# Loading pairs of modulation weights two chunks later in a 1024-chunk weight stream

## What is computed

```python
s_lat = jax.nn.silu(c)
s_ctx = jax.nn.silu(c_ctx)
for layer in range(DEPTH_2):
    shift, scale, gate = jnp.split((s_lat @ ada_w[layer] + ada_b[layer])[:, None, :], 3, axis=-1)
    h = rms_norm(x, pre_g[layer]) * (1.0 + scale) + shift
    ...
    shift_c, scale_c, gate_c = jnp.split(s_ctx @ ada_w[layer] + ada_b[layer], 3)
```

## Time and profile before

| what | value |
|---|---|
| median of 3 runs | 3412.5 us (3409.27 to 3416.88) |
| profiled execution | 3413.3 us, of which the traced span is 3411.5 us |
| mean granted TensorE clock | 0.988 of full |
| PE busy | 3292.8 us, 97% of the span |
| DVE busy, ACT busy | 1537.0 us (45%), 1419.3 us (42%) |
| SP's transfers (queue q1) | 540.08 MB, 48.7% of the DMA engines' time |
| pairs' matmuls | between 590 and 2172 us, and a last block at 2414 us |

### The profile page before, as it was taken

One profiled execution on the slowest core, in us unless ns is written; L12 is line 12 of the kernel. 1 busy time (PEld: TensorE's weight loads), 2 busy tenths in 40 slices (PEclk: granted clock), 3 DMA queues, 4 the chain that ended last, 5 costly groups with the idle time before them and its releaser, 6 DMA issues.

```text
span 3411.5 us, 48332 instructions
## 1 busy us (share of the span) xinstructions
PE 3292.8 (97%) x20802; PEld 2859.4 (84%) x20802; DVE 1537.0 (45%) x1951; ACT 1419.3 (42%) x1962; POOL 32.7 (1%) x30
## 2 busy tenths in 40 slices
PE   7999998999999999999999999999799999999998
PEld 7989998689999987777777778788689888888886
DVE  5444445555555554446232222342544455453554
ACT  5444544544444444447321122232654444444443
POOL 0000002000000000000000000000000000000000
PEclk9999999999999999999999999999899999999999
DMA  6665544756666666665455555443423233232343
GB/s 207 184 189 174 153 151 157 256 189 227 220 225 206 216 227 246 230 231 185 144 173 169 172 171 170 154 141 101 131 81 105 88 102 108 92 106 91 101 136 118
DMA packets 349060, 556.97 MB, mean 163 GB/s; under 512 B 16880, under 2 KB 148976, under 8 KB 347696
## 3 DMA queue, kind: packets, MB, share of 16 engines
q1 hardware_dynamic: 346304, 540.08, 48.7%
q0 software_dynamic: 2256, 13.11, 1.0%
q10 hardware_dynamic: 288, 0.70, 0.1%
HBM read 551.60 MB, written 2.23 MB: 162 GB/s over the span
## 4 chain that ended last, share of the span: by engine, by line
PE 54%; ACT 5%; DVE 4%; issue 2%; DMA 0%; DVEq 0%; ACTq 0%
PE ps L675 48%; PE ps L700 2%; ACT whi L1049 1%; PE ps L868 1%; PE ps L890 1%; ACT hA L1224 1%; PE ps L872 1%; DVE hA L1804 1%; PE ps L886 1%; ACT L1224 1%; DVE hA L1796 1%; DVE wlo L1568 0%; DVE hB L1793 0%; DVE hB L1791 0%; PE ps L731 0%
## 5 line engine op out<-in xcount | busy, mean ns | idle before, releaser
L1568 DVE TENSOR_TENSOR wlo<-raw,whi 128x1024 fp32r<-128x1024 f32 x819 | 999.7, 1228 | 1503.5 <-ACT whi L1049 1496.0
L1049 ACT ACTIVATE whi<-raw 128x1024 fp32r<-128x1024 f32 x824 | 861.8, 1058 | 1395.7 <-PE ps L675 710.6
L675 PE MATMUL ps<-HCh,whi 128*128 128x512 f32 (+1 forms) x1664 | 606.3, 364 | 2.1 <-DVE HCl L1639 2.1
L675 PE MATMUL ps<-HCl,whi 128*128 128x512 f32 (+1 forms) x1664 | 595.3, 358 | 0.0
L675 PE MATMUL ps<-HCh,wlo 128*128 128x512 f32 (+1 forms) x1664 | 595.0, 358 | 0.0
L675 PE MATMUL ps<-Vh,whi 128*128 128x256 f32 x1408 | 403.6, 287 | 12.9 <-DVE wlo L1568 12.8
L675 PE MATMUL ps<-Vh,wlo 128*128 128x256 f32 x1408 | 398.2, 283 | 0.0
L675 PE MATMUL ps<-Vl,whi 128*128 128x256 f32 x1408 | 398.2, 283 | 0.0
L675 PE MATMUL ps<-whi,HCh 128*128 128x256 f32 (+1 forms) x1152 | 377.2, 327 | 1.6 <-DVE HCl L1666 1.5
L675 PEld LDWEIGHTS ps<-HCh,whi 128*128 128x128 f32 x1664 | 316.3, 190 | 71.2 <-issue 21.6
L675 PE MATMUL ps<-wlo,HCh 128*128 128x256 f32 (+1 forms) x1152 | 368.3, 320 | 0.0
(11 more groups left out here) (301 smaller groups left out, 4088.5 us busy)
## 6 DMA issues: line engine op xcount, KB each, us to landing
raw<-in_ada_w SPq DMA_DIRECT2D x192, 512.0 KB, 5.7
raw<-in_w_up SPq DMA_DIRECT2D x176, 512.0 KB, 5.1
raw<-in_w_in SPq DMA_DIRECT2D x160, 512.0 KB, 3.7
raw<-in_od_w_in SPq DMA_DIRECT2D x160, 512.0 KB, 3.5
raw<-in_ev_w_in SPq DMA_DIRECT2D x96, 512.0 KB, 6.2
raw<-in_w_down SPq DMA_DIRECT2D x88, 512.0 KB, 5.1
raw<-in_w_out SPq DMA_DIRECT2D x32, 512.0 KB, 5.2
raw<-in_w_ple_gate SPq DMA_DIRECT2D x32, 512.0 KB, 3.8
```

The source lines that it names most:

```text
L675: mm = e.matmul(o, a, b, start=first and t == 0, stop=last, skip_group_check=True)
L1049: e.activation(m.whi[ch.i % SPLIT][:, 0:n], m.raw[ch.slot][:, 0:n], ACT.Copy).then_inc(S("hi"), 1)
L1568: e.tensor_tensor(m.wlo[ch.i % SPLIT][:, 0:n], m.raw[ch.slot][:, 0:n], m.whi[ch.i % SPLIT][:, 0:n].bitcast(F32), ALU.subtract).then_inc(S( ...
```

## The change

The stream no longer has a pair right behind the main chunk it belongs to. `Plan.group` holds the pair back and appends its two chunks to the stream once two more main chunks have been appended (`LATER = 2`). TensorE still multiplies it where it did. The blocks (`fill`) stay where they were. A split chunk's place is now three split chunks ahead, whatever the stream position, except where the buffer it will use (that of chunk c - 5) held an ada or a raw chunk: then it isn't placed earlier than the main chunk behind which TensorE uses that old chunk (`behind`; for a raw chunk that is the raw chunk itself). The places are now on main chunks alone, so ACT and DVE no longer look for splits at pairs. Two turns of the modulation vectors (`ADA_LAG = 3`, small transposes) are now counted in main chunks rather than in stream positions, two chunks later.

```diff
-ADA_LAG = 3
+ADA_LAG, LATER = 3, 2
...
-    def chunk(self, src, kt, cols, split):
+    def chunk(self, src, kt, cols):
         ch = Chunk()
-        ch.c, ch.src, ch.kt, ch.cols = len(self.chunks), src, kt, cols
+        ch.src, ch.kt, ch.cols, ch.i = src, kt, cols, None
+        return ch
+
+    def stream(self, ch, split=False, behind=None):
+
+        ch.c = len(self.chunks)
         ch.slot, ch.landed = ch.c % RING, 16 * (ch.c // RING + 1)
+        ch.behind = behind or ch
         if split:
...
             at = self.splits[ch.i - AHEAD].c if ch.i >= AHEAD else 0
-            ch.place = -1 if ch.i < 2 else max(at, ch.c - (RING + len(self.filling) - 1))
-        else:
-            ch.i = None
+            old = self.chunks[ch.c - RING] if ch.c >= RING else None
+            ch.place = -1 if ch.i < 2 else max(at, old.behind.c if old and old.i is None else 0)
         self.chunks.append(ch)
-        return ch
...
             rows = W[j * kt * 128:(j + 1) * kt * 128, c0:c0 + cols]
-            at = len(self.chunks)
-            G.chunks.append(self.chunk(rows.rearrange("(k p) c -> p k c", p=128), kt, cols, not raw))
+            ch = self.chunk(rows.rearrange("(k p) c -> p k c", p=128), kt, cols)
+            G.chunks.append(ch)
+            self.stream(ch, not raw)
+            self.mains += 1
+            while self.held and self.held[0][0] <= self.mains:
+                for x in self.held.pop(0)[1].chunks:
+                    self.stream(x, behind=x.behind)
             if fill and j == 2:
-                G.fill = self.ada(fill, at)
-                self.filling = [ch for u in G.fill for ch in u.chunks]
+                G.fill = self.ada(fill)
                 for u in G.fill:
+                    for x in u.chunks:
+                        self.stream(x, behind=G.chunks[0])
                     self.count(*u.chunks)
                 self.count(*G.chunks)
...
-            G.after.append(self.ada(int(self.due), at))
+            G.after.append(self.ada(int(self.due)))
+            self.due -= int(self.due)
             for u in G.after[-1]:
                 self.count(*u.chunks)
-            self.due -= int(self.due)
-            G.turns.append([b for c, b in self.later if at >= c])
-            self.later = [(c, b) for c, b in self.later if c > at]
-        self.filling = []
+                for x in u.chunks:
+                    x.behind = ch
+                self.held.append((self.mains + LATER, u))
+            G.turns.append([b for c, b in self.later if self.mains >= c])
+            self.later = [(c, b) for c, b in self.later if c > self.mains]
...
     def units(self, units):
         for u in units:
-            for ch in u.chunks:
-                self.splits(ch.c)
             self.ada(u)
```

More of the change, by code:

```diff
@@ L68, in __init__ @@
         self.units, self.limit, self.products = 0, 0, 0
-        self.filling, self.later = [], []
+        self.held, self.later, self.mains = [], [], 0
         self.pool_every = 0
         self.n_lo = {"dve": 0, "pool": 0}
-    def chunk(self, src, kt, cols, split):
+    def chunk(self, src, kt, cols):
         ch = Chunk()
-        ch.c, ch.src, ch.kt, ch.cols = len(self.chunks), src, kt, cols
+        ch.src, ch.kt, ch.cols, ch.i = src, kt, cols, None
+        return ch
+    def stream(self, ch, split=False, behind=None):
+        ch.c = len(self.chunks)
         ch.slot, ch.landed = ch.c % RING, 16 * (ch.c // RING + 1)
+        ch.behind = behind or ch
         if split:
@@ L116, in group @@
             elif not fill or j > 2:
-                self.count(G.chunks[-1])
+                self.count(ch)
             self.due += 0 if j in quiet else self.rate
-            G.after.append(self.ada(int(self.due), at))
+            G.after.append(self.ada(int(self.due)))
+            self.due -= int(self.due)
             for u in G.after[-1]:
                 self.count(*u.chunks)
-            self.due -= int(self.due)
-            G.turns.append([b for c, b in self.later if at >= c])
-            self.later = [(c, b) for c, b in self.later if c > at]
-        self.filling = []
+                for x in u.chunks:
[3 more added lines that the diff above has]
+            self.later = [(c, b) for c, b in self.later if c > self.mains]
         G.done = G.chunks[-1].n
@@ L134, in count, with ada @@
             ch.n = self.products
-    def ada(self, n, at):
+    def ada(self, n):
         made = []
@@ L149, in ada @@
             u.chunks = [self.chunk(self.W_ada[l][i * 256:(i + 1) * 256, m * 512:(m + 1) * 512].rearrange(
-                "(k p) c -> p k c", p=128), 2, 512, False) for i in (2 * u.j, 2 * u.j + 1)]
+                "(k p) c -> p k c", p=128), 2, 512) for i in (2 * u.j, 2 * u.j + 1)]
             if u.last and u.batch < 2:
-                self.later.append((at + ADA_LAG, u.batch))
+                self.later.append((self.mains + ADA_LAG, u.batch))
             made.append(u)
@@ L492, in chunks @@
                 self.pump()
-            if j == 2:
-                self.behind(G.fill)
             self.units(G.after[j])
@@ L498, in chunks @@
         return G
-    def behind(self, fill):
-        for u in fill:
-            for ch in u.chunks:
-                self.splits(ch.c)
     def ada_turn(self, b):
```

## The result

| | before | after |
|---|---|---|
| median | 3412.5 us (3409.06 to 3418.1, 7 runs) | 3424.48 us (3419.22 to 3430.54, 7 runs) |
| span of the profiled execution | 3411.5 us | 3422.7 us |
| mean granted TensorE clock | 0.988 | 0.984 |
| PE busy | 3292.8 us | 3297.8 us |

The ratio is 1.0031, 95% interval 1.0021 to 1.004: 12 us slower, 7 to 14 by the interval. Of all executions used here one, in e3, took 4595.13 us at a granted clock of 0.66; no ratio includes it. What the weight loads waited for `wlo` fell as meant, and other waits took its place.

A forecast was written before the change was run, and what follows sets the result against it. TensorE, busy 97% at 0.988 clock, was taken as the bound, so only its standstills or halved clock count. Losses 22.2 + 3.2 + 2.4 = 27.8 against 19.6 gained: 8.2 us slower, 3420.7 us against the median, range 3416 to 3427.

The forecast's parts named there:

- Both shapes of gap: In up, five gaps each from a late cv epilogue and a split behind ACh; all ten go, 14.4 us gained.
- the second shape: In up, as at up2.3: epilogue on time, but a pair moved the split behind ACh; five gaps, forecast gone.
- `down0`: Head of down0: gap shrinks from 3.8 to 1.0 us and the clock drop goes; 2.8 + 2.4 = 5.2 us gained.
- (a): Behind pw2.0 and pw3.0: the pair's transfers lie open and T is late; 11.1 us lost each, 22.2 together.
- The third transfer: Behind pw2.0 and pw3.0: ACT's split ahead of T waits for the third transfer in line, taken as 7.5 us.
- The estimate of 5.6 us for the third of three: At pw2.0 and pw3.0: 512 KB transfers by the skill's fit; 1.9 us less per place, not adopted.
- (b): At bc0.0 and bc1.0: pair's second transfer lands late, too short for the clock; 1.6 us lost each, 3.2 together.
- (c): In ple: pg0.1's split stands ahead of copy E of ple0; 2.4 us lost, clock 0 to 3 more, taken 0.

The follow-up runs named there:

- e3: Changed kernel, but from av0 on each pair again right behind its main chunk in the stream: 3421.33 us, ratio 1.0017 to the kernel before.
- e1: Kernel before with its old stream, only the new split places (and later turns) added: 3426.46 us, ratio 1.0038 to the kernel before.
- e2: Changed kernel's stream, but split places by stream position as before: 3434.88 us, ratio 1.0058 to the kernel before.
- e7: e5 with pairs one main chunk later in the stream instead of two (LATER = 1): 3411.99 us, ratio 0.999 to the kernel before.
- e4: Changed kernel with the splits of bc2.2 and bc3.2 placed at the pw chunk, behind copy T: 3418.83 us, ratio 1.0013 to the kernel before.
- e5: Changed kernel with no split placed ahead of the main chunk behind a raw one: 3420.88 us, ratio 1.0017 to the kernel before.
- e8: Changed stream and places up to down3 only, from ple0 on both as in the kernel before: 3394.75 us, ratio 0.994 to the kernel before.
- e9: e3 with eight splits (bc*.0 and bc*.1) placed as in the kernel before: 3398.96 us, ratio 0.9951 to the kernel before.

## Why the prediction was right, point by point

All the signs named in advance came: no gap over 0.5 us in `up`, about 1 us and a full clock at `down0`, at pw2.0 and pw3.0 a wait for `in_ada_w` and then one for `T` at half the clock, `E` behind a split, and ACT's wait for `in_ev_w_in` at 192.6 us against 373.5.

**Gains.** Both shapes of gap went, for the reason given: ACT no longer waits for a transfer ahead of `cv`, and the split of the second shape stands ahead of `ACh`. That e1 (places alone) removes only the second shape, while the first stays until the pairs stand later (e2, e7), shows that they have two causes. A drift of 1.0 us in the same direction I had not counted. `down0` came as worked out: about 1.0 us of gap forecast, 0.81 found, and the clock kept, -5.3 for -5.2.

**(a) pw2.0 and pw3.0: right in mechanism, 0.9 too high each.** The third transfer took 7.20 us where I took 7.5, the two together 5.83 where I took 5.2; I had 8.7 + 2.4 and found 8.5 + 1.7, the second step being the part behind bc2.0's start. The estimate of 5.6 us for the third of three, worked out from the fit of the Trainium skill ("DMA: Bandwidth & Descriptors", "Anatomy of one DMA — SWDGE (gpsimd) path"), is not borne out by this trace: 7.20 us here, 6.5 and 8.6 by the rows of before. None of these transfers goes over the GpSimd queue that the fit is for. That the raw chunk's buffer is what costs is shown by e3 and e7, where the wait at these pairs goes with the inheritance; that `T` has its part, by e4.

**(b) bc0.0 and bc1.0.** Waits of 1.94 and 1.68 us, for 1.6 forecast, and the clock stayed at 1.00. In e4, the same program up to there, the first of them was 2.65 us and the clock fell to 0.50 behind it, so "too short for the clock" held by a small margin.

**(c) `ple`: a term mis-sized.** The wait is right (2.46 for 2.4). The clock behind it, for which I took 0 from a range of 0 to 3, cost 1.9. The prediction said "Whether a 2.4 us gap lowers the clock, these rows leave open", and one trace doesn't close it: at the same place the clock fell behind 2.32 us in e3 and stayed at 1.00 behind 2.35 us in e1, which lost only 2.5 us there.

**The head of `up0`.** 3.7 us of the traced difference lie here. In every version TensorE waits for the transfers of three pairs of the block. Timelines of PE at the third of them, before and then after, then a window behind it in each (columns as above):

```profile
684.11 1.92 PE L700 MATMUL ps<-raw,Sw 128*24 128x512 f32 x8 [1.40 <-DMA raw<-in_ada_w]
```

```profile
686.19 1.92 PE L703 MATMUL ps<-raw,Sw 128*24 128x512 f32 x8 [3.34 <-DMA raw<-in_ada_w]
```

```profile
688.00:691.00 3.00, 3.00 (x26) 3.00 (x27) 1.81 (x5) 0.95 (x2) 0.00 (x0) 1.00 0.87 320
691.00:694.00 3.00, 3.00 (x16) 3.00 (x16) 0.48 (x1) 0.49 (x2) 0.00 (x0) 0.50 0.53 201
```

The waits make up 1.5 us of the 3.7. The other 2.1 are up0.0 at half the clock, which in the kernel before was back at 1.00 by 688. I can't put a size on any effect of the change here. The changed kernel, e3, e4, e5, e8 and e9 are the same program up to `down3`, and their traces have 3.7, 2.3, 1.3, 0.1, 1.4 and 1.3 us here; e1, e2 and e7 have 3.3, 2.4 and 3.5. All are above zero against the one trace of before, so a part of it may be real; how much stays open. Without it the traces differ by 7.5 us, against 8.2 forecast.

**Where I was lucky.** The forecast held because the changed stream hides the second cost of the new places (`PL`). Nothing in my steps said so: I asked which split stands ahead of `T` and `E`, but not which stands ahead of `PL`, and both experiments built on that (e1, e3) came out some 20 us above what I expected. The closeness of the sum is partly luck too: (a) was 1.8 too high in all and the drift in `up` gave 1.0 more, while `ple` was 2.0 and (b) 0.6 too low.

## What to carry to other kernels

When transfers are reordered in a ring, write out for each chunk whose buffer it inherits, and for each wait of an in-order engine what small copy is queued behind it: both losses here (10.2 us twice, 5 us four times in e3) could be read from those two lists. A delay that helps where pairs are sparse need not be applied where raw chunks hold their buffers until they are multiplied; limiting it to `out`, `up` and `down` gave 20 us, where the same rule over the whole stream lost 12. A place rule and a stream order belong together: neither alone was faster than both together (ratios 1.0038 for e1 and 1.0058 for e2 against 1.0031), though by the intervals only e2 is clearly slower.

## What the runs showed of the hardware

Behind a short wait of TensorE the granted clock fell from 1.00 to 0.50 in some places and not in others, and the length of the wait alone doesn't tell which. In e2 a gap of 1.76 us stands at five places of `up` (up3.2, up7.2, up11.2, up15.2, up19.2); the clock fell behind the first, third and fourth and stayed behind the other two. At ple2.0 it stayed behind 2.35 us (e1) and fell behind 2.32 us (e3). Windows behind up3.2 and up7.2 in e2, then behind ple2.0 in e1 and in e3:

```profile
774.30:777.30 3.00, 3.00 (x17) 3.00 (x16) 2.98 (x3) 1.16 (x2) 0.00 (x0) 0.50 0.68 210
877.30:880.30 3.00, 3.00 (x27) 3.00 (x26) 3.00 (x3) 1.29 (x3) 0.00 (x0) 1.00 0.72 199
1508.50:1511.50 3.00, 3.00 (x8) 1.15 (x7) 1.25 (x2) 2.03 (x3) 0.00 (x0) 1.00 0.10 38
1497.70:1500.70 3.00, 3.00 (x4) 1.13 (x4) 1.22 (x2) 1.97 (x3) 0.00 (x0) 0.50 0.11 41
```

It stayed at 1.00 behind gaps of 0.81 us (down0.3), 1.25 us and 1.94 us (the pair behind bc0.0), and was 0.50 behind 2.12 us (e7) and 2.46 us (`ple`). Where it fell behind gaps of 1.76 to 2.76 us, what followed took 1.5 to 1.8 us longer, so a wait of about 2 us cost 2 us or nearly 4. I had expected the second only of gaps near 4 us, as at `down0`.

Two executions of one stretch of program (the changed kernel and e5 up to `ple`) differed by 3.5 us at the head of `up0`, waits and clock together. Differences of single traces below that, at a place where TensorE waits for several 512 KB transfers in a row, tell little.
